# Input of the first feed-forward: from sixteen TensorE transposes to block transfers with VectorE block transposes

## The reference, cut to what matters

```python
m = mixer(h, w_in[l], b_f[l], conv_w[l], w_branch[l], w_out[l])
x = x + rmsnorm(m, norm_mix_post[l])
h = rmsnorm(x, norm_ffn_pre[l])
f = swiglu(h, w_gate_up[l], w_down[l])      # silu(h @ gate) * (h @ up) @ down
x = x + rmsnorm(f, norm_ffn_post[l])
```

## Time and profile before

| | us |
|---|---|
| median of 3 runs | 962.64 (962.62 to 962.69) |
| the profiled execution's own time | 962.63 |
| its span | 960.9 |
| TensorE busy | 953.6 |
| VectorE busy | 693.7 |
| ScalarE busy | 505.8 |
| GpSimd busy | 20.5 |
| mean granted TensorE clock, share of full speed | 0.999 |

### The profile page before, as it was taken

The page is one execution under the profiler, slowest core; times in us unless marked ns, Lnnn a source line. Parts: engine busy times, 40 slices in busy tenths (PEclk is TensorE's granted clock), DMA queues, the critical chain, the costliest instruction groups (busy, mean ns, idle before and its releaser), DMA issues.

```text
span 960.9 us, 13307 instructions
## 1 busy us (share of the span) xinstructions
PE 953.6 (99%) x5158; PEld 823.2 (86%) x5158; DVE 693.7 (72%) x729; ACT 505.8 (53%) x694; POOL 20.5 (2%) x23
## 2 busy tenths in 40 slices
PE   9999999999999999999999999999999999999997
PEld 8888888888888888888888888899888888888886
DVE  5789758867776768876767676685676587767676
ACT  6544677663434344734343446574978554343434
POOL 1001000040000000000000000000000000000000
PEclk9999999999999999999999999999999999999999
DMA  9845586654555667645555554745445445656551
GB/s 313 252 139 171 181 269 202 223 185 168 190 201 175 218 193 208 211 163 189 198 194 186 184 199 133 234 138 176 158 149 197 132 132 177 216 175 218 175 175 44
DMA packets 138755, 178.75 MB, mean 186 GB/s; under 512 B 25866, under 2 KB 106076, under 8 KB 138588
## 3 DMA queue, kind: packets, MB, share of 16 engines
q1 hardware_dynamic: 138140, 175.86, 55.9%
q10 hardware_dynamic: 576, 2.36, 0.6%
HBM read 175.58 MB, written 1.05 MB: 184 GB/s over the span
## 4 chain that ended last, share of the span: by engine, by line
PE 98%; DVE 1%; ACT 1%; issue 0%; ACTq 0%; DVEq 0%
PE gate_banks L814 13%; PE up_banks L814 12%; PE bank L553 9%; PE bank L554 9%; PE bank L555 9%; PE up_banks L553 7%; PE up_banks L555 7%; PE up_banks L554 7%; PE up_banks L819 7%; PE gate_banks L819 7%; PE up_banks L678 2%; PE up_banks L681 1%; PE bank L736 1%; PE bank L754 1%; PE bank L963 0%; PE bank L889 0%
## 5 line engine op out<-in xcount | busy, mean ns | idle before, releaser
L1837 DVE TENSOR_TENSOR w_lo<-stage,w_hi 128x2048 fp32r<-128x2048 f32 x81 | 185.4, 2289 | 96.5 <-ACT w_hi L1255 96.5
L1831 DVE TENSOR_TENSOR w_lo<-stage,w_hi 128x2048 fp32r<-128x2048 f32 x76 | 173.7, 2288 | 63.9 <-ACT w_hi L1248 63.7
L1248 ACT ACTIVATE w_hi<-stage 128x2048 fp32r<-128x2048 f32 x77 | 147.1, 1912 | 57.7 <-PE up_banks L681 20.6
L1255 ACT ACTIVATE w_hi<-stage 128x2048 fp32r<-128x2048 f32 x81 | 152.5, 1905 | 0.0
L814 PE MATMUL gate_banks<-act_both,w_hi 128*128 128x512 f32 x528 | 129.6, 391 | 0.0
L814 PE MATMUL up_banks<-act_both,w_hi 128*128 128x512 f32 x528 | 125.6, 390 | 0.0
L814 PEld LDWEIGHTS up_banks<-act_both,w_hi 128*128 128x128 f32 x528 | 98.6, 188 | 20.2
L814 PEld LDWEIGHTS gate_banks<-act_both,w_hi 128*128 128x128 f32 x528 | 95.7, 188 | 17.3
L1330 ACT ACTIVATE ffn_hi<-gate 128x512 fp32r<-128x512 f32 x30 | 19.0, 633 | 156.8 <-DVE gate L1967 156.8
L553 PE MATMUL bank<-w_hi,ffn_hi 128*128 128x512 f32 x240 | 93.8, 391 | 0.0
L554 PE MATMUL bank<-w_lo,ffn_hi 128*128 128x512 f32 x240 | 93.7, 391 | 0.0
(11 more groups left out here) (414 smaller groups left out, 1498.6 us busy)
## 6 DMA issues: line engine op xcount, KB each, us to landing
stage<-in_ffn_w SPq DMA_DIRECT2D x66, 1024.0 KB, 5.2
stage<-in_w_in SPq DMA_DIRECT2D x31, 1024.0 KB, 5.2
stage<-in_w_gate_up SPq DMA_DIRECT2D x22, 1024.0 KB, 5.1
stage<-in_w_down SPq DMA_DIRECT2D x11, 1024.0 KB, 4.9
stage<-in_w_out SPq DMA_DIRECT2D x8, 1024.0 KB, 6.4
stage<-in_mem_w_kv SPq DMA_DIRECT2D x8, 1024.0 KB, 5.2
stage<-in_w_branch SPq DMA_DIRECT2D x4, 1024.0 KB, 5.3
stage<-in_mem_w_q SPq DMA_DIRECT2D x4, 1024.0 KB, 5.0
```

What stands on the lines that cost most here:

```text
L1248: act.activation(w_hi[:, place, :], stage[:, place, :], copy).then_inc(hi_done, 1)
L1255: act.activation(w_hi[:, place, :], stage[:, place, :], copy).then_inc(hi_done, 1)
L1831: dve.tensor_tensor(w_lo[:, place, :], stage[:, place, :], w_hi[:, place, :].bitcast(F32), ALU.subtract).then_inc(lo_done, 1)
L1837: dve.tensor_tensor(w_lo[:, place, :], stage[:, place, :], w_hi[:, place, :].bitcast(F32), ALU.subtract).then_inc(lo_done, 1)
```

## The change

The sixteen transposes of `turn_x(S_FFN0, ...)` are taken out. Once `x_n` is complete, sixteen transfers move its 32 x 32 blocks from `x_n` to `v_mem`: each takes one group of 32 partitions of `x_n` (`h`; with its two halves that is 64 tokens) and 32 of every 128 features (`g`), and so consists of 32 x 16 pieces of 128 bytes, 64 KB. SP issues those of three groups of tokens (twelve transfers), ScalarE those of the fourth (four). VectorE turns the blocks into `k_mem` in four block transposes of 128 x 512, and the high and low parts of the input are then made from there instead of from PSUM. The load of chunk 32 goes ahead of SP's transfers; chunk 33's follows them. ScalarE makes the high parts after both reads of the first keys instead of before; VectorE waits for the transfers after `lo(31)`, and has the mean of squares ahead of it. The counts of `x_turned` fall by four for all later users.

```diff
--- before.py
+++ after.py
@@ -173,6 +173,7 @@
         hc_T = v_flat[:, 1024:2048].rearrange("p (j a t) -> p j a t", j=2, a=2)
         mem_blocks = v_flat.rearrange("p (k n) -> p k n", k=KD)
         k_flat = k_mem[:, :, :].rearrange("p a b -> p (a b)")
+        x_T = k_flat.rearrange("p (t k n) -> p t k n", t=2, k=KD)
         z_T = k_flat[:, 0:4 * (T + 2)].rearrange("p (a t) -> p a t", a=4)
         y_T = k_flat[:, 1040:1040 + 2 * T].rearrange("p (a t) -> p a t", a=2)
         gate_c, gate_a = (gate[:, 8 * i:8 * i + 8, :].rearrange("p a b -> p (a b)").rearrange("p (t d) -> p t d", t=2)
@@ -261,6 +262,7 @@
         kscaled_done, keys_landed, k_done = sem("kscaled_done"), sem("keys_landed"), sem("k_done")
         zeroed, par_turned, par_ready = sem("zeroed"), sem("par_turned"), sem("par_ready")
         x_turned, x_done = sem("x_turned"), sem("x_done")
+        x_blocks_landed, x_blocks_turned = sem("x_blocks_landed"), sem("x_blocks_turned")
         act_hi_done, act_lo_done = sem("act_hi_done"), sem("act_lo_done")
         aux_done, aux_free = sem("aux_done"), sem("aux_free")
         dqsum_done, dqdev_done = sem("dqsum_done"), sem("dqdev_done")
@@ -366,6 +368,17 @@
             for at in range(0, P, 32):
                 rows(BF, 1, a["b_f"], 8, at)
 
+        def x_blocks(engine, rows_):
+            for h in rows_:
+                tokens_ = slice(32 * h, 32 * h + 32)
+                for g in range(4):
+                    r = slice(32 * g, 32 * g + 32)
+                    engine.dma_start(v_flat.rearrange("p (a n) -> p a n", n=P)[r, :, tokens_],
+                                     x_n[tokens_, :, :].rearrange("i t d -> i (t d)").rearrange("i (a f) -> i a f", f=P)[:, :, r]
+                                     ).then_inc(x_blocks_landed, 16)
+
         def store(engine, t, j):
             cols = slice(512 * j, 512 * j + 512)
             engine.dma_start(out[0, P * t:P * t + P, cols], m_n[:, t, cols]).then_inc(stored, 16)
@@ -412,7 +425,8 @@
                     rows(c + i, w, 512 * i, 4, col, 512, slot(c + i))
 
             def feed_forward(base, w_g, g_col, w_u, u_col, w_d, between=None):
-                whole(base, w_g, g_col, slot(base))
+                if base != FFN[0]:
+                    whole(base, w_g, g_col, slot(base))
                 whole(base + 1, w_u, u_col, slot(base + 1))
                 with sp.Fori(0, PAIRS - 2) as t:
                     c = base + 2 + t * 3
@@ -504,6 +518,10 @@
                                      raw_k[32 * (tb % 4):32 * (tb % 4) + 32, tb // 4, :].rearrange("i (k f) -> i k f", k=KD)[:, :, r]
                                      ).then_inc(keys_landed, 16)
 
+            whole(FFN[0], a["w_gate_up"][0], 0, slot(FFN[0]))
+            sp.wait_ge(memt_turned, 4)
+            sp.wait_ge(x_done, 4 * S_FFN0 + 4)
+            x_blocks(sp, (0, 1, 2))
             feed_forward(FFN[0], a["w_gate_up"][0], 0, a["w_gate_up"][0], HID, a["w_down"][0], key_blocks)
             token_pair(MEMV[0], a["mem_w_kv_2"][0], D)
             feed_forward(FFN[1], a["ffn1_w1_2"][0], 0, a["ffn1_w3_2"][0], 0, a["ffn1_w2_2"][0])
@@ -1031,8 +1049,6 @@
 
             pe.wait_ge(mem_lo_done, 8)
             up_tok(MEMK, mix_hi, mix_lo, 0)
-            turn_x(S_FFN0, 0)
-            turn_x(S_FFN0, 1)
             up_tok(MEMK, mix_hi, mix_lo, 1)
             tokens(MEMK + 2, mix_hi, mix_lo)
 
@@ -1257,7 +1273,7 @@
             def gained(gains, col, turned, after, blocks=range(KD)):
 
                 for b in blocks:
-                    act.wait_ge(x_turned, 4 + 4 * turned + b // 2 + 1)
+                    act.wait_ge(x_turned, 4 * turned + b // 2 + 1)
                     if b == 0 and after:
                         act.wait_ge(used, after)
                     act.activation(act_hi[:, b, :], pair[ACC + b // 2][:, b % 2, :], copy,
@@ -1519,10 +1535,16 @@
             deviation(N_POST0)
             hi(30)
             squares(N_FFN0, S_FFN0)
-            gained(par, G_FFN_PRE, 1, OUT1 + 4)
+            act.wait_ge(memt_turned, 4)
+            x_blocks(act, (3,))
             key_read(0, 0)
             hi(31)
             key_read(0, 1)
+            act.wait_ge(used, OUT1 + 4)
+            for b in range(KD):
+                act.wait_ge(x_blocks_turned, b // 4 * 2 + 2)
+                act.activation(act_hi[:, b, :].rearrange("p (t n) -> p t n", t=2), x_T[:, :, b, :], copy,
+                               scale=par[:, G_FFN_PRE + b:G_FFN_PRE + b + 1]).then_inc(act_hi_done, 1)
             deviation(N_FFN0)
             hi(32)
             hi(33)
@@ -2205,9 +2227,19 @@
             lo(29)
             after_norm(N_POST0, S_FFN0, 1)
             lo(30)
-            gained(par, G_FFN_PRE, 2)
+            mean_square(N_FFN0)
             lo(31)
-            mean_square(N_FFN0)
+            dve.wait_ge(x_blocks_landed, 16 * 16)
+            dve.wait_ge(mem_lo_done, 8)
+            for part in (0, 2, 1, 3):
+                at = slice(512 * part, 512 * part + 512)
+                dve.transpose(k_flat[:, at], v_flat[:, at]).then_inc(x_blocks_turned, 1)
+            for b in range(KD):
+                dve.wait_ge(act_hi_done, 16 + b // 2 * 2 + 2)
+                dve.scalar_tensor_tensor(act_lo[:, b, :].rearrange("p (t n) -> p t n", t=2), x_T[:, :, b, :],
+                                         par[:, G_FFN_PRE + b:G_FFN_PRE + b + 1],
+                                         act_hi[:, b, :].bitcast(F32).rearrange("p (t n) -> p t n", t=2),
+                                         ALU.mult, ALU.subtract).then_inc(act_lo_done, 1)
             inverse(N_FFN0)
             spread(N_FFN0)
             lo(32)
```

## The result

| | before | after |
|---|---|---|
| median, us (22 runs each) | 962.63 (962.19 to 962.74) | 963.83 (963.31 to 965.51) |
| the profiled execution's own time, us | 962.63 | 965.04 |
| its span, us | 960.9 | 963.3 |

The ratio is 1.0017, with a 95% interval of 1.0011 to 1.0023: the changed kernel is slower, by 1.2 us, a difference so small that it can only just be told. The runs of the changed kernel are not spread evenly. Fourteen lie between 963.31 and 963.98, eight between 965.01 and 965.51, with none between. The profiled execution is one of the eight.

What follows compares the result with a forecast made beforehand. TensorE was taken as the bound, busy 953.6 of 960.9 us. Removing transposes gives -1.76, standing still before the gate product +2.8, together +1.1 on 962.63: 963.7 us, range 961.4 to 967.0.

Steps and rivals of the forecast that it cites:

- the forecast case: Blocks land at 194.5 to 195.9 us, giving a kernel time of 963.2 to 964.6 us; chance 0.40.
- The removal: Sixteen transposes before the gate product cost TensorE some 1.76 us on the path; at most that is gained.
- The chain from landing to the gate product: VectorE transposes, ScalarE scalings and chunk 32's high and low parts let TensorE start 9.2 us after landing.
- rival A: Blocks drain as they are issued and land at 193.9 or earlier: 962.6 us, down to 960.9; chance 0.20.
- my early bound: Blocks landed at 193.9: SP's last transfer starts at 191.9, steps of 0.66, plus 1.9 us to landing.
- rival B: Issuing 512 pieces on SP takes longer than 256; a doubled step of 1.31 gives 969.7 us; chance 0.14.
- my own case: TensorE stands still 2.8 us before the gate product, shorter than 3.6 us, so its clock stays at full speed.
- the bound for "slower": Kernel time over 964.6 us, slower by over 0.2%; chance 0.39.
- My six named cases: The forecast landing and five rivals, with chances 0.40, 0.20, 0.14, 0.16, 0.05 and 0.05.
- the rule: Transfers within SBUF reach 78% of top rate at 128 bytes, so engines keep up with issues: 962.6 us.
- rival E: SP's and ScalarE's issues take turns, the sixteen transfers following one another: +2.6, or 965.2 us; chance 0.05.
- Rival D: ScalarE's four issues are slow and TensorE waits at the key product: 964 to 965 us; chance 0.05.

Runs made afterwards that it cites:

- e5: Edit of e2: VectorE makes chunk 32's low part between its transposes and the input's low parts, not before the wait for the blocks; 960.87 us, ratio 0.9982.
- e1: Changed kernel without the sixteen transfers and the wait for them, the input made from the memory's old blocks; 962.14 us, ratio 0.9993.
- e4: Changed kernel with SP and ScalarE issuing eight transfers each in place of twelve and four; 965.26 us, ratio 1.0026.
- e3: Changed kernel with ten 128 x 128 identity matmuls issued where TensorE stands still before the gate product; 963.78 us, ratio 1.0013.
- e6: Changed kernel with the low part of chunk 32 computed twice, so TensorE stands still longer; 968.09 us, ratio 1.0055.
- e2: Changed kernel with high and low part of chunk 32 made ahead of the input and of the wait for the blocks; 961.55 us, ratio 0.9989.
- e7: The changed kernel measured once more without an edit; 963.83 us, ratio 1.0015.

## Why the prediction was right, and where it was not

**The sum.** 963.7 us was forecast, 963.83 measured, inside the forecast case. The mechanism came as forecast: the transposes' time was taken off TensorE's path, and the chain behind the landing made TensorE wait longer than that. How near the number came is in part luck, as the next two points show. The removal was worth 1.76 as read: e5 has it whole (1.78). The chain from landing to the gate product was 9.1 us for the forecast 9.2, in the changed kernel and in e1. The gate product started at 204.03 for 204.2, TensorE waited 2.5 us for 2.8.

**The landing: right number, wrong reason.** I had 195.0 from the DMA engines (166 GB/s behind chunk 32) over 193.9 from the issues. Measured was 194.9, and the issues set it. The 166 GB/s was a misreading of the earlier trace rows. In finer slices of that same microsecond of the kernel before (40 slices, busy tenths and GB/s), and over its first 0.65 us alone:

```profile
DMA  9999999999999999999999999999787787644444
...
DMA packets 957, 0.13 MB, mean 200 GB/s; under 512 B 941, under 2 KB 957, under 8 KB 957
```

The engines were full only for the first part, at 200 GB/s; then they ran short of pieces, and the mean of 166 holds that too. At 200 GB/s my own sum gives 188.7 + 5.2 = 193.9 for the engines, no later than the issues, and thus 962.6 us, rival A. What made up for it were the issues, about 1.0 us over my early bound: eleven steps of 0.67 for 0.66, one of them 0.7 longer (an issue of 1.32 instead of 0.63), and 2.1 us to landing instead of 1.9. Nor did the blocks stand strictly behind chunk 32, as I had it: the load landed 7.5 us after its issue instead of 7.0, with small pieces moving beside it. Twice the pieces per transfer cost 0.02 us at the issue (0.63 against 0.61), so rival B's doubled step was rightly kept out. The engines' limit is not far: in e4 it is at 194.1.

**The clock: the step that failed.** "In my own case the standing still is shorter than that and the clock stays" holds in 14 of 22 runs. In the other eight, by the groups, it fell, after a wait of 2.5 us, where the end of the kernel before had shown it at 3.6 us. I took that single event as a threshold. e3 (the pause filled, no group at 965.2) and e6 (a longer pause, all four runs) show that it is the pause. The fallen clock costs 1.6 us in a third of the runs, so the mean lies 1.6 us over before instead of 1.0. The median hides this because fewer than half of the 22 runs are affected: with more than half it would have been about 965.1, over my forecast case and over the bound for "slower".

**The chances.** My six named cases already add up to 1.00, so the 0.03 for "faster" was no remainder, and a landing between 193.9 and 194.5 belonged to no case. The measured landing lies in neither gap.

**Small pieces and two queues.** In the full stretch this trace shows 198 to 200 GB/s for 128-byte pieces, against 387 GB/s for the pieces of a weight load at 186 to 187 us, which is 52% of it. The Trainium skill (DMA: Bandwidth & Descriptors, "Why small descriptors are slow (HBM only)") gives its 78% for a remote transfer of 1 MB, measured against the link's top rate. For these copies within one core's SBUF the trace doesn't agree. What the prediction drew from the rule came true all the same: 200 GB/s was enough for the engines to catch up with the issues by 191.

SP's and ScalarE's issues ran side by side, ScalarE's at 0.71 and SP's at 0.63 in the median, so rival E was rightly small. The Trainium skill (Perfetto Trace Analysis, "DMA Instruction — HWDGE (DVE, Sync)") tells of one descriptor generator that is locked for exclusive use; by this trace such a lock can't last the whole issue.

**ScalarE's issues.** I set them behind the squares, at 185.8. They started at 184.62, while the squares were still running, and the first key read began at 187.95, as soon as its product was ready. Rival D had no ground at four issues. At eight (e4) it came true: 1.9 us of waiting at the key product.

**The queues behind.** Chunk 33's load started at 193.5 for 192.6 and was covered, as said; in the profiled execution nothing after the gate product waited that had not waited before. But the cover further on was thin: e2 ran out of it at the down product once the gate product was 1.76 us earlier. My sum took "everything is shifted as a whole" for granted; it holds for a later start, not for an earlier one.

## What to carry to other kernels

Work taken off the bounding engine is worth its time only if the new way to the same data ends before that engine arrives; add up the chain from the last input to the consumer, and look what else stands on it by mere order: here 4.2 us of weight preparation, which engines that stood idle could have done first, made the difference between 963.8 and 960.9 us. A wait on TensorE can cost more than its length, here 1.6 us on top of 2.5, and only in some of the runs; when a changed kernel's times fall in two groups, look at the granted clock behind the wait. A mean over a window says what full engines can move only if they are full to its end; look at finer slices before you use it as a rate. And an engine that finishes earlier spends slack further down: after a gain of a microsecond or two, look for the next wait.

## What the runs showed of the hardware

- By the groups, the clock fell around a wait of TensorE of 2.5 us in 13 of 33 runs of the changed kernel, in all four at 4.9 us (e6), and in none of the ten at 1.0 us (e1). Three of these executions with a fallen clock were profiled. It can fall within the wait (at about 203.8 in the changed kernel's profile) or after the work has resumed (e7); the gate product took 1.6 us longer in the one and 1.7 in the other.
- The time of an issue hardly depends on the pieces: 0.63 us for 512 of 128 bytes, 0.61 for 256. But single issues stall, 1.32 us on SP and, in e4, 1.16 on SP and 1.19 on ScalarE, ending within 0.4 us before the load ahead of them lands; why is not shown.
- 128-byte pieces from SBUF to SBUF move at about 200 GB/s in the full stretch, about half of the 387 GB/s that the 1 KB pieces of a weight load reach.
- A DMA issue of ScalarE can start while its earlier activations are still running: the first one started at 184.62, the last square ended at 185.87.
